# Closing stage of each layer: the add of the two row sets of the expert sums moved from VectorE to GpSimd, issued two tiles ahead

## What is computed

```
f = _moe(tokens, router_w[l], router_b[l], exp_w_gate[l], exp_w_up[l], exp_w_down[l],
         sh_w_gate[l], sh_w_up[l], sh_w_down[l])
x = x + g2 * _rms_norm(f[:n_lat].reshape(bsz, s_len, dm), post_ffn_g[l])
if with_ctx:
    xc = xc + g2c * _rms_norm(f[n_lat:].reshape(bsz, -1, dm), post_ffn_g[l])
```

## Time and profile before

| | us |
|---|---|
| median of 3 runs (lowest, highest) | 2919.43 (2918.8, 2921.94) |
| the profiled execution | 2917.33 |
| its span in the profile | 2915.5 |
| TensorE busy, share of the span | 2595.9, 89% |
| VectorE busy | 1081.1, 37% |
| ScalarE busy | 588.0, 20% |
| GpSimd busy | 390.1, 13% |
| layer 0's closing stage, first load's issue to the end of the last residual add | 1596.52 to 1628.65 |
| layer 1's, the same | 2887.78 to 2912.07 |

### The profile page before, as it was taken

One profiled execution on the slowest core, in us unless ns is written; L12 is line 12 of the kernel. 1 busy time (PEld: TensorE's weight loads), 2 busy tenths in 40 slices (PEclk: granted clock), 3 DMA queues, 4 the chain that ended last, 5 costly groups with the idle time before them and its releaser, 6 DMA issues. The chain is left out here.

```text
span 2915.5 us, 44582 instructions
## 1 busy us (share of the span) xinstructions
PE 2595.9 (89%) x13635; PEld 1267.2 (43%) x13636; DVE 1081.1 (37%) x3197; ACT 588.0 (20%) x1379; POOL 390.1 (13%) x312
## 2 busy tenths in 40 slices
PE   7999989896899999999996588989978999899894
PEld 3566555543433333333332266666533333333331
DVE  3443360515333333333332643451433332233233
ACT  2323241402011111111111341331310111111111
POOL 1000001001022222221221200001010212112212
PEclk9999999997999999999998799999989999999997
DMA  7120303007478998999993402202156999998983
GB/s 275 50 91 30 130 12 132 32 13 287 169 236 301 353 327 284 324 325 334 328 367 81 188 1 90 87 34 96 37 215 235 361 397 392 389 391 297 388 313 106
DMA packets 104979, 619.27 MB, mean 212 GB/s; under 512 B 22832, under 2 KB 23088, under 8 KB 64688
## 3 DMA queue, kind: packets, MB, share of 16 engines
q1 hardware_dynamic: 71184, 530.30, 46.2%
q0 software_dynamic: 33696, 87.63, 12.3%
HBM read 578.84 MB, written 77.99 MB: 225 GB/s over the span
## 5 line engine op out<-in xcount | busy, mean ns | idle before, releaser
L1513 PE MATMUL ps<-wgu,xT 128*64 128x512 f32 x3584 | 808.0, 604 | 43.1 <-DMA wgu<-in_exp_gu 34.2
L1513 PEld LDWEIGHTS ps<-wgu,xT 128*64 128x64 f32 x3584 | 253.8, 139 | 502.2 <-issue 492.2
L1522 PE MATMUL ps<-wd,hiddenT 128*64 128x512 f32 x1824 | 420.3, 603 | 11.2 <-issue 10.8
L624 PE MATMUL ps<-w_in,hT 128*128 128x512 f32 (+5 forms) x1152 | 369.0, 479 | 14.7 <-PEq L574 3.8
L1442 POOL DMA_INDIRECT ffn_rows<-Y,six x114 | 182.6, 1602 | 1110.8 <-issue 635.3
L1695 DVE TENSOR_TENSOR hidden<-silu,ps 128x256 f32<-128x256 f32 x112 | 47.2, 421 | 704.3 <-ACT silu L1631 698.5
L624 PEld LDWEIGHTS ps<-w_in,hT 128*128 128x128 f32 x1152 | 218.0, 196 | 155.7 <-issue 136.0
L1522 PEld LDWEIGHTS ps<-wd,hiddenT 128*64 128x64 f32 x1824 | 123.2, 137 | 227.7 <-issue 227.7
L1631 ACT ACTIVATE silu<-ps 128x256 f32<-128x256 f32 x112 | 43.1, 385 | 797.7 <-PE ps L1513 797.7
L1626 ACT ACTIVATE Y<-ps,wc 128x512 f32<-128x512 f32 x114 | 78.4, 688 | 417.4 <-PE ps L1522 417.4
L1689 DVE TENSOR_SCALAR Y<-ps,wc 128x512 f32<-128x512 f32 x114 | 85.6, 751 | 198.4 <-PE ps L1522 198.4
(11 more groups left out here) (490 smaller groups left out, 2724.1 us busy)
## 6 DMA issues: line engine op xcount, KB each, us to landing
wgu<-in_exp_gu SPq DMA_DIRECT2D x128, 2048.0 KB, 22.9
wd<-in_exp_d SPq DMA_DIRECT2D x128, 1024.0 KB, 8.2
ada_start<-in_ada_w SPq DMA_DIRECT2D x8, 1024.0 KB, 8.0
w_in<-in_w_in SPq DMA_DIRECT2D x4, 2048.0 KB, 10.8
w_in<-in_w_out SPq DMA_DIRECT2D x4, 2048.0 KB, 12.4
aw_0A<-in_ada_w SPq DMA_DIRECT2D x6, 1024.0 KB, 4.8
aw_0B<-in_ada_w SPq DMA_DIRECT2D x6, 1024.0 KB, 4.8
aw_0C<-in_ada_w SPq DMA_DIRECT2D x6, 1024.0 KB, 4.8
```

The source lines that it names most:

```text
L624: last = pe.matmul(pp[i % 2][:, at:at + c1 - c0], hT[:, k, i * P:(i + 1) * P], wg[g % 2][:, k, c0:c1], start=(k == 0), stop=(k == KD - 1))
L1513: last = pe.matmul(ps[h * HB:(h + 1) * HB, 0, :], xT[:, k, h * HB:(h + 1) * HB], wgu[w[h]][:, k, :], start=(k == 0), stop=(k == KD - 1))
L1522: last = pe.matmul(ps[h * HB:(h + 1) * HB, 1 + c, :], G[:, f, h * HB:(h + 1) * HB], wd[w[h]][:, f, c * 512:(c + 1) * 512], start=(f == 0), ...
```

## The change

GpSimd makes the ten adds in place of VectorE. Its list becomes: add 0, add 1, and then for each i: add i+2 (if there is one), power i. VectorE's list becomes: mean square 0, the wait for the gate row, and for each i: mean square i+1, scaling i, residual add i. The semaphores are the same and count the same; the loads, ScalarE's list and SyncE's list are unchanged. In the changed file the add is L1786, the power L1794 and the mean square L1802.

```diff
@@ -1781,7 +1781,15 @@
 
             @block.gpsimd
             def _(pool):
-                for i in range(nt):
+                def add_halves(i):
+                    s_f[i].wait(pool, 32)
+                    pool.tensor_tensor(f[:, i, :], f[:, i, :], f2[:, i, :], ALU.add).then_inc(s_sum.sem, 1)
+
+                add_halves(0)
+                add_halves(1)
+                for i in range(nt):
+                    if i + 2 < nt:
+                        add_halves(i + 2)
                     s_ms.wait(pool, i + 1)
                     pool.tensor_tensor(ss[:, 2, i:i + 1], ss[:, 1, i:i + 1], v.half[:, 0:1], ALU.pow).then_inc(s_rstd.sem, 1)
 
@@ -1793,17 +1801,9 @@
                     s_sq.wait(dve, i + 1)
                     dve.tensor_scalar(ss[:, 1, i:i + 1], ss[:, 0, i:i + 1], 1.0 / D, EPS, ALU.mult, ALU.add).then_inc(s_ms.sem, 1)
 
-                def add_halves(i):
-                    s_f[i].wait(dve, 32)
-                    dve.tensor_tensor(f[:, i, :], f[:, i, :], f2[:, i, :], ALU.add).then_inc(s_sum.sem, 1)
-
-                add_halves(0)
-                add_halves(1)
                 mean_square(0)
                 s_row.wait(dve, 16)
                 for i in range(nt):
-                    if i + 2 < nt:
-                        add_halves(i + 2)
                     if i + 1 < nt:
                         mean_square(i + 1)
                     s_rstd.wait(dve, i + 1)
```

## The result

| | before | changed |
|---|---|---|
| median of 19 runs (lowest, highest), us | 2920.47 (2913.29, 2925.76) | 2926.66 (2921.62, 2936.93) |
| the profiled execution | 2917.33 | 2933.62 |
| layer 0: add of tile 2 to the end of the last residual add | 19.66 | 24.09 |
| layer 1: the same | 12.35 | 15.02 |

The ratio is 1.0022, with a 95% interval of 1.0015 to 1.003: slower by 6.4 us, between 4.4 and 8.8 (the two medians alone differ by 6.2). The two stretches of the last rows, in which the change acts, are longer by 4.43 and 2.67 us, 7.1 together. About half of that, 1.69 and 1.70 us, is the first scaling that starts later; the other 3.7 us are four tiles that take 4.54 to 4.61 us where they took 3.65. The forecast was +9.1 and 2928.5 us.

The account below looks back on a forecast made before the run. The closing stages, uncovered by other work, were bound by tile 2's DMA landing, then VectorE's instructions. Layer 0's +6.0 and layer 1's +3.1 us gave +9.1 on 2917.33, 2926.4; plus 2.1 for the median, 2928.5 us; range 2923 to 2932.

Parts of the forecast that it names:

- The signs that were named: Closing stages: residual adds or scalings of 3.2 to 3.5 us, three in layer 0, one in layer 1.
- Part 1: Closing stages: adds of tiles 0 and 1 cost nothing; removing the six behind tile 2's landing gains at most 6.8 us.
- Part 2: Price of a 128x1024 add on Pool: 2.3 us taken, with 2.21 and 2.62 as ends.
- Part 3: Start of the closing chain: power 0 queues behind add 2 on Pool, so scaling 0 begins 1.7 us late per layer.
- Part 4: Pool add beside a VectorE instruction with two SBUF inputs: each excludes the other, VectorE waiting the whole rest of the add.
- rival (b): Closing stages: both engines run side by side, Pool pacing a tile at 2.85 us; +0.2 us, 2919.6 us; chance 0.10.
- Part 5: Closing-stage tile with an add beside it: 5.1 us against 3.65; layer 0 +6.0 us, layer 1 +3.1 us.
- (a): Closing stages: only Pool waits, VectorE always passes, 4.0 us a tile; +4.9 us, 2924.3 us; chance 0.12.

Follow-up runs that it names:

- pool_first_two: Kernel before with only the adds of tiles 0 and 1 on Pool: 27.33 and 19.52 us from add 0, 19.67 and 12.36 from add 2.
- pool_power_first: Changed kernel with power 0 ahead of add 1 on Pool and tile 0's scaling and residual add ahead of mean square 1: 32.70 and 22.47 us from add 0.
- pool_add_behind_scaling_b: Changed kernel with Pool's adds from tile 3 on waiting for the scaling of the tile in front: 26.27 and 15.71 us from add 2.

## Why the prediction was right

The time, 2926.66 us, lies in the range (2923 to 2932) and 1.8 us from the forecast; against a before of 2920.47 the change cost 6.4 us where 9.1 were expected. "Slower by over 0.2%" had 0.77; with an interval of 0.15 to 0.30% the result lies close to that line, and the size was too large by 2.7 us. The time fits better than the size for a reason that is luck: the forecast stood on a median before of 2919.43 us from 3 runs, and that of 19 runs is 1.0 higher, which took 1.0 off the miss.

The signs that were named came: scalings of 3.30 to 3.37 us, three in layer 0 and one in layer 1, with all others at 1.27 or 1.28. From the start of scaling 0 to the end of layer 1's last residual add it is 12.1 us, where 12.6 was written.

**Part 1, right.** The adds of tiles 0 and 1 cost nothing where they are (pool_first_two).

**Part 2, right.** The Pool add with VectorE out of the way takes 2.34 us; 2.3 was taken.

**Part 3, right.** Scaling 0 starts 2.91 and 2.90 us behind the start of add 2, against 1.21 before: 1.70 us late in layer 1 and 1.69 in layer 0.

**Part 4, right, and by the reason given.** The trace of before showed only that Pool waits for VectorE. The other half, that VectorE waits for Pool, was taken from the same exclusive use, and the scaling of 3.37 us shows it. The Trainium skill (SBUF — State Buffer, Who interferes with whom) has it in the same detail as the runs: two SBUF inputs on VectorE against any Pool read (an add of 2.06 us in place of 1.22 beside a copy), no conflict with at most one SBUF input outside the two-port modes (1.29 beside an add), none with a Pool write (1.22 beside a memset). It says that the one that comes second "fully blocks"; by the trace the scaling ends 1.09 us behind the add's row where it takes 1.27 alone. Whether VectorE is let in 0.18 us early or does the first part of its instruction while it waits is not told apart.

The text says that VectorE had nothing to do in both long Pool adds. That is wrong for layer 1's, and the row would have helped:

```profile
1976.81 8.31 POOL L607 TENSOR_TENSOR TD_1D<-TD_1D,cst 128x3840 f32<-128x3840 f32 x1 [160.78 <-DMA TD_1D<-in_bias]
...
1984.47 0.42 DVE L893 COPY KT_1D<-ps 128x256 f32<-128x256 f32 x1 [10.33 <-PE ps L648]
```

A VectorE copy out of PSUM lies wholly inside the Pool add and takes 0.42 us, as the same copy does in layer 0 behind the end of that layer's add. So the trace of before held a VectorE instruction without an SBUF input that is not kept out; of one with two it says nothing. The note in the Trainium skill (Advanced Engine Details and Errata, VectorE Performance Modes), read as complete, would have given rival (b), +0.2 us; it was rightly outweighed by the 1.52 us of the powers.

**Part 5, the step that was mis-sized.** The text says that after VectorE's start of scaling 0 "Pool's next read comes some 0.15 us after its start, so VectorE is first", 5.1 us a tile. Pool was first, each time. In the first tile of each layer the add started 0.05 us ahead of the scaling; in the other two tiles of layer 0 it had been waiting since 0.86 us before the scaling, behind the residual add (1624.69 against 1625.55). The one lag of that size in the rows is the 0.16 us of the powers, and a power waits for a mean square that VectorE issues just ahead of its scaling. The add of tile 3 waits for nothing on VectorE; its rows have landed, and it only stands behind power 0 in its own list. With Pool first the text had 4.8; measured are 4.61 and twice 4.54. What waits ends sooner behind the other than its own length: the scalings end 1.09 us behind the add, not 1.27, and the adds that waited end 2.19 us behind the residual add, not 2.34. The four tiles with an add differ by 4 x 5.1 - (4.61 + 4.54 + 4.54 + 4.61) = 2.1 us, which is all of the 2.0 by which 9.1 exceeds the 7.1 of the two stretches. The order that the prediction had assumed (scaling, then the Pool add, then the residual add) occurs in tile 0 of each layer of pool_power_first, with residual adds of 3.25 and 3.24 us. pool_add_behind_scaling_b has VectorE first at the scaling and at the residual add too, and takes 5.28 us a tile.

**The rivals.** (a), only Pool waits, is out by the 3.37 us. (b), side by side, does not hold for this kernel but is what one gets once VectorE's second operand leaves SBUF: 18.92 and 13.25 us from add 2, where rival (b)'s working gives 1627.95 - 1608.99 = 18.96 and 2912.95 - 2899.72 = 13.23.

That the remaining 0.7 us between 7.1 (the stretches) and 6.4 (the ratio) means anything is not shown; the interval covers both.

## What to carry to other kernels

Moving an instruction from VectorE to Pool frees VectorE only if the two can run at once: with two SBUF inputs on one side and a Pool read on the other they take turns, and the time is nearly the sum of both engines' work, with Pool's share at about twice the price (2.34 us an add against 1.22). Before such a move, look at an existing Pool row beside a VectorE row: a 0.55 us power that takes 1.52 us is the warning. One SBUF input is not always harmless: beside the normalising of L425, which reads one 128x1024 tile in SBUF and one column, and takes 0.74 us, the power took 0.99 us. If the move is still wanted, give VectorE one operand in PSUM (here a copy of the gate row, and the scaled tile), and look for work that fits into the wait for the DMA ahead of it.

## What the runs showed of the hardware that was not expected

- An exclusion can leave no trace in the lengths of the engine that loses by it: with VectorE always first, all its rows were 1.22 to 1.28 us and the closing stages were the longest of all. The loss stood in 2.67 us of idle time a tile behind a power that was queued on Pool; about 1 us of it is the exclusion, the rest the added wait.
- Scaling and residual add of 128x1024 cost the same with operands in PSUM: 1.28 and 1.22 us against 1.27 and 1.22.
- Where a small Pool instruction falls has a price too: a power that starts inside a residual add with both inputs in SBUF takes 1.46 us and, with no other work on VectorE to cover it, costs VectorE 0.44 us.
